# Mixture-of-experts layer: expert rows added to their tokens by a weighted one-hot matmul in PSUM, and expert weights read from memory in longer runs

## What is computed

```python
def hier_moe(x, w_group, w_expert, w_gate, w_up, w_down):   # 32 experts, 2 for each token, 512 hidden columns
    ...                                                     # routing: weight and expert_id for each of 512 (token, choice)
    def expert_block(args):
        xb, e = args
        h = jax.nn.silu(xb @ w_gate[e]) * (xb @ w_up[e])
        return h @ w_down[e]
    yb = lax.map(expert_block, (rows, block_expert)).reshape(P, d)
    out = jax.ops.segment_sum(yb * row_w[:, None], row_tok, num_segments=T + 1)[:T]
    ...
x = layer_norm(DEEPNORM_ALPHA * x + hier_moe(...), ln_ffn_g, ln_ffn_b)   # as the kernel has it
```

## Time and profile before

| | |
|---|---|
| median of 3 runs | 2484.46 us |
| the profiled execution: its time, and its span | 2484.86 us, 2483.1 us |
| PE busy, mean granted clock | 85%, 0.844 |
| DVE, ACT, POOL busy | 27%, 13%, 7% |
| weights of the two MoE layers | 64 experts x 6 MB, by L112, L1088 and L1102 |
| first MoE layer, from its first matmul to that of the next block | 302.58 to 866.42 us |

### The profile page before, as it was taken

How to read it: one execution, slowest core, us unless ns; L and a number is a source line. 1 busy time by engine, 2 the same in 40 slices (tenths; PEclk the granted TensorE clock), 3 DMA queues, 4 the chain that set the end, 5 groups by cost and what they waited for, 6 DMA issues and landing times. The chain is left out here.

```text
span 2483.1 us, 33384 instructions
## 1 busy us (share of the span) xinstructions
PE 2119.0 (85%) x13513; PEld 1427.3 (57%) x13513; DVE 667.5 (27%) x2009; ACT 313.5 (13%) x841; POOL 175.2 (7%) x224
## 2 busy tenths in 40 slices
PE   8999789888877498679878888488889989889997
PEld 7776466556555344366555555244478734448863
DVE  4354321111111315421111111328432112833211
ACT  2122000000000013100000000012322101222100
POOL 0112101000000100000000000100001100000110
PEclk9999867777888697767777777689899999989999
DMA  9333459999999742259999999852144342212420
GB/s 335 125 129 109 128 210 396 395 394 395 394 392 393 288 159 95 85 208 363 395 395 395 395 395 394 302 201 102 38 145 142 142 169 103 101 68 102 169 85 25
DMA packets 246122, 574.69 MB, mean 231 GB/s; under 512 B 13316, under 2 KB 16634, under 8 KB 245534
## 3 DMA queue, kind: packets, MB, share of 16 engines
q1 hardware_dynamic: 242974, 569.46, 62.0%
q0 software_dynamic: 3072, 4.21, 0.5%
HBM read 568.39 MB, written 9.44 MB: 233 GB/s over the span
## 5 line engine op out<-in xcount | busy, mean ns | idle before, releaser
L981 PE MATMUL ps<-ring,arena 128*32 128x256 f32 x3968 | 301.8, 469 | 107.6 <-DMA ring<-in_moe_w_up_dram 55.9
L981 PEld LDWEIGHTS ps<-ring,arena 128*32 128x32 f32 x3968 | 169.9, 135 | 250.5 <-issue 207.6
L2097 PE MATMUL ps<-arena,ring 128*128 128x256 f32 x1408 | 304.4, 379 | 1.6 <-DVE arena L244 1.6
L2097 PEld LDWEIGHTS ps<-arena,ring 128*128 128x128 f32 x1408 | 267.4, 190 | 38.5 <-DVE arena L244 2.3
L959 PEld LDWEIGHTS ps<-arena,h 128*128 128x128 f32 x2112 | 256.4, 202 | 29.5 <-issue 26.4
L959 PE MATMUL ps<-arena,h 128*128 128x32 f32 x2112 | 264.0, 286 | 3.0 <-DVE arena L949 3.0
L1394 PE MATMUL ps<-ring,arena 128*128 128x512 f32 (+1 forms) x576 | 250.9, 595 | 2.4 <-DVE arena L244 1.6
L1021 PE MATMUL ps<-ring,arena 128*32 128x256 f32 x1984 | 212.0, 602 | 38.1 <-issue 37.0
L266 PE MATMUL ps<-ring,arena 128*128 128x512 f32 x544 | 239.0, 602 | 1.6 <-DVE arena L1434 0.8
L1394 PEld LDWEIGHTS ps<-ring,arena 128*128 128x128 f32 x576 | 110.1, 193 | 136.2 <-issue 132.4
L266 PEld LDWEIGHTS ps<-ring,arena 128*128 128x128 f32 x544 | 104.8, 193 | 133.2 <-issue 130.4
(11 more groups left out here) (295 smaller groups left out, 1781.5 us busy)
## 6 DMA issues: line engine op xcount, KB each, us to landing
ring<-in_moe_w_gate_dram SPq DMA_DIRECT2D x62, 2048.0 KB, 19.4
ring<-in_moe_w_up_dram SPq DMA_DIRECT2D x62, 2048.0 KB, 22.4
ring<-in_moe_w_down_dram SPq DMA_DIRECT2D x62, 2048.0 KB, 19.8
ring<-in_w_up_dram SPq DMA_DIRECT2D x22, 2048.0 KB, 7.8
ring<-in_ssm_w_in_dram SPq DMA_DIRECT2D x12, 2048.0 KB, 12.2
ring<-in_w_in_dram SPq DMA_DIRECT2D x10, 2048.0 KB, 11.7
ring<-in_w_down_dram SPq DMA_DIRECT2D x10, 2048.0 KB, 7.8
ring<-in_attn_w_qkv_dram SPq DMA_DIRECT2D x6, 2048.0 KB, 20.2
```

What stands on the lines that cost most here:

```text
L981: mm = nc.tensor.matmul(ps[j * CAP:(j + 1) * CAP, 2 + b, 0:256], xg[:, b, k * CAP:(k + 1) * CAP], w[:, k, (j % 2) * 256:(j % 2 + 1) * 256] ...
L2097: mm = nc.tensor.matmul(ps[:, n % 4, 0:SEQ], w[:, k, k4 * P:(k4 + 1) * P], xT_mlp[:, k, :], start=(k == 0), stop=(k == KD - 1))
```

## The change

The weights are read so that each partition takes adjacent rows of the matrix: gate and up are one run of 16 KB for each partition instead of eight of 2 KB, and down two runs of 8 KB instead of four of 4 KB. Sums over the contraction come in another order for that, so `h_rows` holds `h` with its columns arranged to match (ACT, once per layer), and the transposes take every second column.

The stores, `moe_rows`, the waits for them, `pairs` and the destination step are gone. The rows of four experts are collected in `y` (128 x 1024, two copies of 32 x 256 on ACT and two on DVE for each expert). `step_back` builds on DVE, for these four experts, a one-hot matrix with the routing weight as its value; PE transposes it (`step_back_turn`), ACT copies it (`step_back_copy`), and `step_combine` adds `y` to the tokens in PSUM banks 0 to 3 with four 128x512 matmuls (calls). These banks begin with ALPHA times `h`, four matmuls of the same size in expert 0. Statistics and norm read PSUM. The other steps have one PSUM bank each instead of two. The last expert has no `step_pick`.

```diff
-                add(cols8(t["moe_w_gate"][layer, e], 0, FF))
-                add(cols8(t["moe_w_up"][layer, e], 0, FF))
-                add(rows4(t["moe_w_down"][layer, e], 0))
+                add(t["moe_w_gate"][layer, e].rearrange("(p k) n -> p k n", p=P))
+                add(t["moe_w_up"][layer, e].rearrange("(p k) n -> p k n", p=P))
+                add(t["moe_w_down"][layer, e].rearrange("(a p k) n -> p a k n", a=2, p=P))
...
-                        nc.tensor.matmul(ps[:, b, k * CAP:(k + 1) * CAP], h[:, tt, k * P:(k + 1) * P],
-                                         slots[:, b, tt, 0:CAP], start=(tt == 0), stop=(tt == TT - 1))
-                for tt in range(TT):
-                    mm = nc.tensor.matmul(ps[:, b, KD * CAP:KD * CAP + 2], slots[:, b, tt, :],
-                                          info[:, tt, bass.ds(e, 1), :].rearrange("p a b -> p (a b)"),
-                                          start=(tt == 0), stop=(tt == TT - 1))
+                        mm = nc.tensor.matmul(ps[:, 4, k * CAP:(k + 1) * CAP], h_rows[:, tt, k, :],
+                                              slots[:, b, tt, :], start=(tt == 0), stop=(tt == TT - 1))
...
+            def step_rows_act(act, s, v, read, i, y=y):
+                act.wait_ge(s["down"].sem, v(s["down"]))
...
+                for j in range(2):
+                    ins = nc.scalar.activation(y[i * CAP:(i + 1) * CAP, j * 256:(j + 1) * 256],
+                                               ps[j * CAP:(j + 1) * CAP, 7, 0:256], ACT.Copy)
+                ins.then_inc(s["rows_act"].sem, 1)
...
+            def step_back(dve, s, used, e0, n, back=back):
...
+                for i in range(n):
+                    for tt in range(TT):
+                        ins = nc.vector.tensor_scalar(back[:, tt, i * CAP:(i + 1) * CAP],
+                                                      cst[:, C_IOTA4:C_IOTA4 + CAP], pos1[:, tt, bass.ds(e0 + i, 1)],
+                                                      wtok[:, tt, bass.ds(e0 + i, 1)], ALU.is_equal, ALU.mult)
+                ins.then_inc(s["back"].sem, 1)
...
+            def step_combine(pe, s, rows_done, back_done, n, last=False, y=y, backT=backT):
+                pe.wait_ge(s["back_copied"].sem, back_done)
+                pe.wait_ge(s["rows_act"].sem, rows_done)
+                pe.wait_ge(s["rows_dve"].sem, rows_done)
+                for tt in range(TT):
+                    for half in range(2):
+                        mm = nc.tensor.matmul(ps[:, 2 * tt + half, :], backT[0:n * CAP, tt, :],
+                                              y[0:n * CAP, half * 512:(half + 1) * 512], start=False, stop=last)
...
-                    for b in range(2):
-                        sp.wait_ge(y_st[b].sem, 16 * (NE // 2))
-                    for tt in range(TT):
-                        sp.dma_start(pairs[:, tt, :, :].rearrange("p j d -> p (j d)"),
-                                     moe_rows[layer][8 * P * tt:8 * P * (tt + 1), :].rearrange(
-                                         "(p j) d -> p (j d)", p=P)).then_inc(pairs_loaded.sem, 16)
...
+                        if not is_last(q, i):
+                            step_pick(pe, m, next_views(q, i)[1], 1 - b)
+                        if i == 0:
+                            if peeled:
+                                pe.wait_ge(alpha_ready.sem, alpha_ready.at(1))
+                                for tt in range(TT):
+                                    for part in range(2):
+                                        nc.tensor.matmul(ps[:, 2 * tt + part, :], alpha_id,
+                                                         h[:, tt, part * 512:(part + 1) * 512], start=True, stop=False)
+                            else:
+                                step_combine(pe, m, m["rows_act"].at(4 * q), m["back_copied"].at(q), 4)
+                        if i == 2:
+                            pe.wait_ge(m["back_copied"].sem, m["back_copied"].at(q + 1))
+                        step_turn(pe, m, v, b)
...
+                        step_down(pe, m, v, before, b, w[2])
+                        if i == 1:
+                            step_back_turn(pe, m, m["back"].at(q + 1), 4)
...
+                    for tt in range(TT):
+                        ins = nc.scalar.activation(h_rows[:, tt, :, :], h[:, tt, :].rearrange("p (n k) -> p k n", k=KD),
+                                                   ACT.Copy)
+                    ins.then_inc(h_arranged.sem, 1)
...
+                        read = None if first_quad(q) else q
+                        if i == 2:
+                            step_back_copy(act, m, m["back_turned"].at(q + 1), read, 4)
+                        step_rows_act(act, m, v, read, i)
...
-                    dve.wait_ge(pairs_loaded.sem, pairs_loaded.at(32))
                     for tt in range(TT):
-                        V(nc.vector.scalar_tensor_tensor(h[:, tt, :], h[:, tt, :], ALPHA, pairs[:, tt, 0, :],
-                                                         ALU.mult, ALU.add))
-                    for tt in range(TT):
-                        V(nc.vector.tensor_tensor(h[:, tt, :], h[:, tt, :], pairs[:, tt, 1, :], ALU.add))
-                        dve_stats(tt)
-                    dve_layer_norm(dve, lnp)
+                        dve.wait_ge(token_combined.sem, token_combined.at(tt + 1))
+                        for half in range(2):
+                            nc.vector.bn_stats(ln_stats[:, tt, half, :], ps[:, 2 * tt + half, :])
+                    dve_layer_norm(dve, lnp, True)
```

More of the change, by code:

```diff
@@ L916, in moe @@
             hT = area(4460, 2, 2, 2 * CAP)
-            rows = area(4716, 2, 256)
-            pos1 = area(5228, TT, NECOL)
-            info = area(5300, TT, NECOL, 2)
+            back = area(4716, TT, P)
+            backT = area(4972, TT, P)
+            pos1 = area(5228, TT, NE)
+            wtok = area(5300, TT, NE)
             chosen = area(5440, TT, 2, NE)
@@ new lines, in step_back_turn, with step_back_copy @@
+            def step_back_turn(pe, s, ready, n, back=back):
+                pe.wait_ge(s["back"].sem, ready)
+                for tt in range(TT):
+                    mm = nc.tensor.transpose(ps[0:n * CAP, 6, 128 + tt * P:128 + (tt + 1) * P], back[:, tt, 0:n * CAP],
+                                             ident)
+                mm.then_inc(s["back_turned"].sem, 1)
+            def step_back_copy(act, s, ready, read, n, backT=backT):
+                act.wait_ge(s["back_turned"].sem, ready)
+                if read is not None:
+                    act.wait_ge(o["combined"].sem, read)
+                nc.scalar.activation(backT[0:n * CAP, :, :], ps[0:n * CAP, 6, 128:128 + TT * P]
+                                     .rearrange("p (a b) -> p a b", a=TT), ACT.Copy).then_inc(s["back_copied"].sem, 1)
@@ L1156, in _, with expert @@
                     pe.wait_ge(route_dve.sem, route_dve.at(5))
-                    def expert(pair, b):
-                        e, v, prev, before = pair_view(pair, b)
-                        peeled = isinstance(pair, int) and pair == 0
-                        in_arena = peeled and b == 1
-                        half, turn = (0, 0) if peeled else (1 - b, pair - 1 + b)
+                    def expert(q, i):
+                        e, v, prev, before = views(q, i)
+                        b, peeled = i % 2, first_quad(q)
+                        half, turn = (0, 0) if peeled and e == 0 else (1 - b, 2 * q + i // 2 - 1 + b)
+                        in_arena = peeled and e == 1
                         w = w1 if in_arena else wf[half]
@@ new lines, in expert @@
+                        if i == 1:
+                            step_back_turn(pe, m, m["back"].at(q + 1), 4)
+                    pe.wait_ge(h_arranged.sem, h_arranged.at(1))
+                    step_pick(pe, m, lambda s: s.at(1), 0)
+                    for i in range(4):
+                        expert(0, i)
+                    with pe.Fori(1, QUADS - 1) as q:
+                        for i in range(4):
+                            expert(q, i)
+                    for i in range(4):
+                        expert(QUADS - 1, i)
```

290 lines of the change are left out of this document (142 added, 148 removed).

## The result

The changed kernel takes 2364.36 us (median of 4 runs, 2363.42 to 2373.56), the kernel before 2484.69 in the same session. The ratio is 0.9525, 95% interval 0.95 to 0.9549: faster, by 120 us. The forecast was 2390 with a range from 2368 to 2426. So the sign was right, the gain was larger than the 94.9 us worked out, and the time lies 3.6 us under the range.

The account below looks back on a forecast made before the run. In the two MoE layers weights were taken to set the pace, or nearly, with PE close behind. Layer gains of 48.1 and 46.8, together 94.9, off 2484.9 gave 2390 us, range 2368 to 2426.

Parts of the forecast that it names:

- Longer runs: Expert weight loads: 16 KB runs at 428 GB/s and 8 KB at 422, 14.76 us per expert in place of 16.13.
- Rival 1: DMA gains nothing by longer runs, only the stores' time goes: 2448 us, chance 0.10.
- DMA's own length: Weight stream, S to G: 27 x 14.76 + 9.8 + 8.5 for latency and gaps = 416.8 us.
- S to G: End of expert 2's gate and up to start of expert 31's: 454.8 and 453.0 us before, 420 forecast.
- PE's own path: PE's work and waits, S to G: 374.1 + 35 + 9.6 = 418.7 us, 14.6 per expert.
- the wait at `i == 2`: PE's turn in one of four experts waits for ACT's copy: 1.2 us, 8 times, 9.6 in all.
- nearly equal streams: PE at 418.7 and DMA at 416.8 us cost each other a little, so 420 was taken.
- rival 3: PE and waits cheap, DMA binds early: 411 to 416.8 us and smaller gaps, 2372 to 2383; chance 0.13.
- Rival 2: PE becomes the bound outright as its clock falls: 15.0 us per expert gives 2411, 15.5 gives 2440; chance 0.22.
- Rival 4: Slower, PE at its low level through the layer: 20.8 us per expert, 2747; this or another loss, chance 0.05.
- Before S: Layer start to end of expert 2's gate and up: added matmuls less removed L962 groups, net loss 2.6 us per layer.
- End of the layer: Start of expert 31's gate and up to next block: 30.4 and 29.0 us against 46.3 and 45.4, gains 15.9 and 16.4.

Follow-up runs that it names:

- Run 3: Kernel before with the new weight layout and `h_rows` alone, stores and `pairs` kept: 2419.14 us, ratio 0.9743.
- run 2: Changed kernel with the weights in the old runs of 2 KB and 4 KB, no `h_rows`: 2430.87 us, ratio 0.9804.
- run 6: Changed kernel loading one eighth of gate and up and half of down from expert 3 on: S to G 380.2 and 378.0 us.
- Run 8: Changed kernel with few weight bytes, each combine inside the loop moved from ahead of the turn to behind down: S to G 397.9 and 393.6 us.
- run 5: Kernel before, loading one eighth of gate and up and a quarter of down from expert 3 on: S to G 385.7 and 390.7 us.
- run 7: Changed kernel with few weight bytes, each combine but the last cut to one 128x32 matmul: S to G 367.1 and 367.1 us.
- again: The changed kernel unaltered, run once more for its time and a second profile: 2362.87 us, ratio 0.9531.
- run 11: Changed kernel with experts 0 and 1 in the ring at the layer's start and expert 2 in the arena: 2361.68 us, ratio 0.9522.

## Why the prediction was right in direction and too high

**Longer runs: right.** The windows gave 14.76 us per expert, and from expert 11 on the changed kernel takes 14.76 or 14.77 per expert in the first layer (means of four), but for the last four with 14.86. The plateaus, gate, up and down together, move at 426, which is what 6.291 MB in 14.76 us come to. No window was taken of 16 KB runs alone, so the 428 for these stays an estimate. Run 3 shows the same rate with the stores still there. The Trainium skill (DMA: Bandwidth & Descriptors, Specifications) has transfers from 512 B on at line rate; runs 2 and 3 contradict that for these loads, 394 against 426 by the layout alone. Its 425 GB/s (Bandwidth, Measured) is within 2 of what these plateaus show (424 to 427). Rival 1 is out.

**DMA's own length: a little too long.** This is what sets S to G. 27 x 14.76 + 9.8 = 408.3; measured 413.9. So latency and gaps were 5.6, where I carried 8.5 over from before.

**PE's own path: the step that failed.** "Sum: 374.1 + 35 + 9.6 = 418.7 us, 14.6 per expert. So PE and DMA come out almost equal" is wrong: alone PE takes 380.2 and 378.0 (run 6). The sum added durations at the clock of the kernel before, and had no term for what the change does to that clock. Of the 39.6 us too many (418.7 less 379.1):
- the combine was priced at its duration, 4.5, and is worth 1.9 and 1.6 net at its place: 7 x 4.5 less 12.0 is 19.5. Run 8 shows that 4.5 is about right elsewhere; the row of L1394 gave the cost of the instruction, not what it does for its neighbours.
- the rest of an expert, turn, down and gate and up, was kept at what it took in the kernel before, and takes 0.5 us less (runs 5 and 7): some 14 over the stretch. The rise of the clock behind it is measured (0.75 to 0.80), its cause isn't.
- the wait at `i == 2` was 0.75, not 1.2: 9.6 less 8 x 0.75 is 3.6.
- the base: 390 against 388.2 (run 5): 1.8.
- L962, taken at 0.55, was worth 0.57: 0.6 the other way.

Some 1.3 of it stay unaccounted for. With this, nothing of the "nearly equal streams" is left: of PE and DMA, DMA alone sets S to G. The 420 taken for S to G is 6.1 too much. 3.2 of these come from PE's path, without which DMA's own 416.8 would have stood, and 2.9 from DMA's latency and gaps. "PE and waits cheap, DMA binds early" was the condition of rival 3, which so had the mechanism right, though its time of 2372 to 2383 was too high as well, because it kept my figures for both ends. Rival 2 is out, since PE alone needs 13.2 us per expert and not 15.0. Its clock did not fall but rose, 0.85 from 420 to 780 us in `again` against 0.78 in the same window before. Rival 4 is out as well.

**Before S: wrong in sign.** Forecast a loss of 2.6 per layer, measured a gain of 2.3 and 2.1. In the changed kernel's second layer (`again`) ALPHA times `h` (L1209) and what follows are

```profile
1031.43 3.68 PE L1209 MATMUL ps<-h,arena 128*128 128x512 f32 x8
1035.04 0.68 PE L1002 MATMUL ps<-cst,arena 64*128 64x64 f32 x4
1036.20 1.94 PE L1020 MATMUL ps<-ring,arena 128*32 128x256 f32 x32 [0.48 <-DVE arena L1010]
```

and in the kernel before

```profile
1097.46 0.59 PE L962 MATMUL ps<-arena 128*128 128x2 f32 x4
1097.98 0.66 PE L1004 MATMUL ps<-cst,arena 64*128 64x64 f32 x4
1099.19 3.26 PE L1021 MATMUL ps<-ring,arena 128*32 128x256 f32 x32 [0.56 <-DVE arena L1012]
```

Dense work stands ahead of a down again: 3.68 us instead of 4.5, and 1.3 given back by the down. Against the kernel before, pick and turn of expert 0 come 3.1 us further apart (7.20 against 4.11), and what is behind them to S is 3.1 us shorter (another L962 gone, and the high level for the most part). So what the added calls cost is made up behind them. The gain comes from ahead of them: L962 gone at the low level (0.8), and gate and up of expert 0 in 4.95 us instead of 6.08. These stand before L1209 and owe it nothing; why the level rises earlier there isn't shown. Of the two gains the second layer's is the steady one: that layer takes 62.7 to S in runs 3 and 5, built on the kernel before, and 60.4 to 60.6 in all runs with the change. The first layer has no such steady value: 59.0 in runs 3 and 5 and 62.74 in the profile before, 57.2 to 66.8 with the change. So its 2.3 belongs to these two executions. In the first profile shown, where gate and up of expert 0 take 6.42 and L1209 6.2, S comes 6.3 us later than in `again`.

**End of the layer: right in kind.** Forecast 30.4 and 29.0, measured 25.4 and 27.5. The statistics end 13.7 us behind G in both layers, not 16.6: the combine took 3.67 of the 4.5, down 1.93 of 3.4. In the first layer the block ends 11.7 us behind the statistics instead of 13.8. There the next block starts 0.5 us after POOL's end (803.04 to 803.54), where the kernel before took 3.1 (863.28 to 866.42); why isn't shown. In the second layer it is 13.8, and "here SP is next in line" came true: POOL ends at 1492.62, SP's issue at 1494.78, which is G + 27.1 where I had 27.4, and the next block starts at 1495.2. There SP costs some 2 us.

Added up, S to G has 12.1 more gain than forecast (6.4 by PE's path and 5.7 by DMA's latency), the stretch before S 9.6 and the end 6.5, less 2.2 outside: 26.0, which is 120.9 less 94.9. So PE's path is the step that was most wrong, but what it adds to the miss directly is a quarter of it. The same step, work priced at the clock of before, stands behind 2.3 of the end's 6.5 (combine and down of the first layer) and behind a part of the 9.6. Without the 9.6 before S, of which a part is the luck of these two executions, the time would have been about 2374, within the range. The sign and the larger part of the gain rest on steps that held, the longer runs and the shorter end.

## What to carry to other kernels

Price a step that is added to TensorE between short or thin matmuls together with what stands right behind it. A group of dense 128x512 matmuls that takes 5.38 us by itself cost 1.6 to 1.9 net ahead of a turn and a down, which then ran at the high level. The same group cost about 4 behind the down, and a second one 3.4 to 3.5 where the level was high already. And when a kernel's clock swings, don't carry the time of the untouched instructions over as a constant. Where two streams come out equal in a forecast, take each one's bytes or work away alone: it tells in one run which has room. And make a chunk's adjacent bytes long in memory before anything else is tuned around a stream that binds: that alone gave half of this gain.

## What the runs showed of the hardware

- Runs of 2 KB and 4 KB move at 394 GB/s and runs of 16 KB and 8 KB at 426, for the same bytes on the same queue.
- The same 32 records of down take 1.93 us behind a whole combine and 3.64 behind a small one, in all 14 cases of runs 6 and 7; the same combine takes 3.67 to 6.35 in the profiles of the changed kernel.
- With few bytes PE is busy for 247 to 251 of 260 us (runs 5 to 7), and yet its granted clock is 0.75 to 0.83: it swings between its two levels with hardly any idle time.
- Executions of one kernel differ by up to 17 us (run 11: 2351.47 to 2368.66). In the changed kernel's two profiles most of the difference is the stretch before S.
